# TensorE passes eight stage meetings without waiting, and issues 21 idle matmuls at three waits

## What is computed

```python
h = h + 0.5 * swiglu(rmsnorm(h, g), wg, wu, wd)
h = h + even_mixer(rmsnorm(h, mix_g), ...)      # layer 0; layer 1: odd_mixer
h = h + memory_xattn(rmsnorm(h, mg), rmsnorm(mem, sg), wq, wkv, qg, kg, wo)
h = h + 0.5 * swiglu(rmsnorm(h, g2), wg2, wu2, wd2)
```

## Time and profile before

| | |
|---|---|
| median of three runs | 1660.08 us (1658.35 to 1664.02) |
| profiled execution: time, span | 1660.82 us, 1659.0 us |
| TensorE busy | 1612.4 us, 97% of the span |
| VectorE busy | 1018.5 us, 61% |
| ScalarE busy | 863.3 us, 52% |
| mean granted TensorE clock | 0.996 of full |
| chain that ended last: share of TensorE | 87% |

### The profile page before, as it was taken

One profiled execution on the slowest core, in us unless ns is written; L12 is line 12 of the kernel. 1 busy time (PEld: TensorE's weight loads), 2 busy tenths in 40 slices (PEclk: granted clock), 3 DMA queues, 4 the chain that ended last, 5 costly groups with the idle time before them and its releaser, 6 DMA issues.

```text
span 1659.0 us, 21003 instructions
## 1 busy us (share of the span) xinstructions
PE 1612.4 (97%) x8524; PEld 1364.0 (82%) x8524; DVE 1018.5 (61%) x1379; ACT 863.3 (52%) x1193; POOL 33.7 (2%) x35
## 2 busy tenths in 40 slices
PE   9989999999999999999899999999999999999998
PEld 8878877999888888877777888888888888778887
DVE  5565578698755554568866555455544775765543
ACT  5365675566545443555666444354434565654441
POOL 0000002000000000002000000000000000000000
PEclk9999999999999999999999999999999999999999
DMA  7742324765544555544243655555554533435543
GB/s 286 289 167 108 127 104 176 286 225 189 183 178 178 180 185 193 178 152 153 71 159 130 222 181 180 201 177 178 188 192 178 178 127 127 152 128 190 191 178 127
DMA packets 42959, 289.95 MB, mean 175 GB/s; under 512 B 5048, under 2 KB 5198, under 8 KB 9968
## 3 DMA queue, kind: packets, MB, share of 16 engines
q1 hardware_dynamic: 38272, 271.93, 45.5%
q0 software_dynamic: 4592, 16.69, 2.9%
HBM read 287.51 MB, written 8.55 MB: 178 GB/s over the span
## 4 chain that ended last, share of the span: by engine, by line
PE 87%; DVE 6%; ACT 3%; DMA 2%; issue 1%; DVEq 0%; PEldq 0%; SPq 0%; ACTq 0%; POOL 0%; PEld 0%
PE bank L481 26%; PE bank L483 26%; PE bank L482 25%; PE bank L487 5%; DVE low L447 2%; DMA raw<-stream_dram 2%; PE bank L763 1%; ACT high L436 1%; PE bank L1401 1%; PE bank L645 1%; DMA h<-x_dram 0%; PE bank L1989 0%; PE bank L1843 0%; DVE h L1182 0%; DVE prob L1796 0%
## 5 line engine op out<-in xcount | busy, mean ns | idle before, releaser
L447 DVE TENSOR_TENSOR low<-raw,high 128x2048 fp32r<-128x2048 f32 x254 | 581.2, 2297 | 376.6 <-ACT high L436 376.0
L436 ACT ACTIVATE high<-raw 128x2048 fp32r<-128x2048 f32 x256 | 486.9, 1913 | 350.3 <-DMA raw<-stream_dram 345.6
L481 PE MATMUL bank<-high,xh 128*128 128x512 f32 (+1 forms) x1232 | 486.1, 395 | 6.5 <-DVEq L2720 3.5
L483 PE MATMUL bank<-high,xl 128*128 128x512 f32 (+1 forms) x1232 | 477.8, 388 | 0.0
L482 PE MATMUL bank<-low,xh 128*128 128x512 f32 (+1 forms) x1232 | 477.1, 387 | 0.0
L481 PEld LDWEIGHTS bank<-high,xh 128*128 128x128 f32 x1232 | 232.1, 188 | 54.7 <-DVE low L447 4.6
L483 PEld LDWEIGHTS bank<-high,xl 128*128 128x128 f32 x1232 | 231.9, 188 | 48.4
L482 PEld LDWEIGHTS bank<-low,xh 128*128 128x128 f32 x1232 | 232.3, 189 | 44.5
L481 PE MATMUL bank<-high,hh 128*128 128x512 f32 x440 | 171.9, 391 | 0.0
L483 PE MATMUL bank<-high,hl 128*128 128x512 f32 x440 | 171.3, 389 | 0.0
L482 PE MATMUL bank<-low,hh 128*128 128x512 f32 x440 | 171.2, 389 | 0.0
(11 more groups left out here) (242 smaller groups left out, 1522.2 us busy)
## 6 DMA issues: line engine op xcount, KB each, us to landing
raw<-stream_dram SPq DMA_DIRECT2D x257, 1024.0 KB, 4.8
band_wide_dram<-band_rows_dram POOLq DMA_DIRECT2D x1, 3072.0 KB, 33.4
t_wide_dram<-t_rows_dram POOLq DMA_DIRECT2D x1, 2304.0 KB, 17.1
u<-mem_dram POOLq DMA_DIRECT2D x2, 1024.0 KB, 5.1
bias<-band_wide_dram POOLq DMA_DIRECT2D x1, 2048.0 KB, 14.3
rel_wide_dram<-rel_rows_dram POOLq DMA_DIRECT2D x1, 1920.0 KB, 17.1
bias<-t_wide_dram POOLq DMA_DIRECT2D x1, 1536.0 KB, 10.7
bias<-rel_wide_dram POOLq DMA_DIRECT2D x1, 1280.0 KB, 7.0
```

Source lines behind the costliest of these rows:

```text
L436: act.activation(self.high[:, n % RING, :], self.raw[:, n % RING, :], ACT.Copy).then_inc(self.high_split, 1)
L447: dve.tensor_tensor(self.low[:, n % RING, :], self.raw[:, n % RING, :], self.high[:, n % RING, :].bitcast(F32), ALU.subtract).then_inc(sel ...
L481: pe.matmul(out, lh, rh, start=start, stop=False)
L483: return pe.matmul(out, ll, rh, start=False, stop=stop)
```

## The change

Idle matmuls are issued on TensorE behind the latent projection (8), and in `Rope` behind the first turn (5) and the second (8).

TensorE does not wait at the meeting in front of eight stages: the seven that follow residual sums with an early turn, and the odd attention. It still drains and adds its one to `stage_done`. Instead it waits for the semaphores that it needs: that GpSimd has cleared the set (`cleared`), that the early tiles are copied (`early_low`), and behind the first `k` of products that all four quarters are summed (`sum_added`). The tiles 4 and 5 are turned behind the products of `k` = 0, tiles 6 and 7 behind those of `k` = 1. In front of the odd attention it waits for the drained rows and copies of the earlier jobs. VectorE splits the second weight slot ahead of the low halves of tiles 4 to 7. ScalarE's order is as before.

```diff
     def begin(self, pe, s):
+        if self.early:
+            return
         self.tensor(pe, s, 0, self.early + self.AHEAD)
+    def after(self, pe, s, k):
+        if self.early and 2 * k < KT - self.early:
+            if k == 0:
+                pe.wait_ge(self.core.sum_added, self.sums_needed)
+            self.tensor(pe, s, self.early + 2 * k, self.early + 2 * k + 2)
     def next(self, pe, s, k):
+        if self.early:
+            return
     def arrive(self, pe, s, k):
+        if self.early and k == 0:
+            pe.wait_ge(self.core.early_low, self.early_needed)
...
         if self.source:
+            if self.source.early:
+                c.split_low(dve, self.jobs[0][0].slot(self.jobs[0][1]) + 1 - LEAD)
             self.source.lows(dve, s)
...
+        keep_clock(pe, c, self.idle)
+        if self.leads:
+            self.rows_there(pe, s, len(self.jobs) - 2)
+            pe.wait_ge(s["turned_by_act"], self.turn.drained("act", len(self.turn.by) - 1))
...
+        core.split_low(dve, self.up.first + 1 - LEAD)
         self.rows.lows(dve, s)
-        core.split_low(dve, self.up.first + 1 - LEAD)
...
             self.turn_rows(pe, s, b)
+            keep_clock(pe, self.core, (5, 8)[b])
...
+    def meet(engine, n, wait=True):
         engine.drain().then_inc(core.stage_done, 1)
+        if not wait:
+            return
...
             for n, stage in enumerate(stages):
+                if stage.ahead:
+                    pe.wait_ge(core.cleared, n - 1)
                 stage.tensor(pe, core.sets[n % 2])
-                meet(pe, n)
+                meet(pe, n, wait=n + 1 == len(stages) or not stages[n + 1].ahead)
...
                     pool.sem_clear(range(other[0], other[-1] + 1))
+                    pool.drain().then_inc(core.cleared, 1)
```

More of the change, by code:

```diff
@@ L497 @@
 class Stage:
+    ahead = False
     def __init__(self, core):
@@ L745, in __init__ @@
         self.early = 0
+        self.sums_needed = None
         self.step = 2 if base == 0 and tiles == KT and gain is None else 1
@@ L748, in __init__, with begin_early @@
         self.gain = PARAM(core.param, "gains")[:, n:n + KT] if gain else None
-    def begin_early(self):
+    def begin_early(self, early_before, sums_needed):
         self.early, self.banks = 4, tuple(range(8))
+        self.early_needed, self.sums_needed = early_before + self.early, sums_needed
     def bank(self, k):
@@ L791, in early_lows @@
             dve.wait_ge(s["next_high"], k + 1)
-            self.low(dve, k).then_inc(s["next_low"], 1)
+            self.low(dve, k).then_inc(self.core.early_low, 1)
     def tensor(self, pe, s, first=0, end=KT):
@@ L952, in __init__ @@
     def __init__(self, core, x, jobs, loads=None, source=None, scale=False, batches=None,
-                 masked=0, select=None, ending=False, by_act=(), behind=()):
+                 masked=0, select=None, ending=False, by_act=(), behind=(), idle=0):
         super().__init__(core)
+        self.idle = idle
         self.ending = len(jobs) - 1 if ending else None
@@ L960, in __init__ @@
         self.select = select
+        self.leads = False
         self.masked = masked
@@ L986, in tensor @@
         xh, xl = self.x
-        if self.source:
+        if self.source and not self.source.early:
             self.source.tensor(pe, s)
@@ L1003, in tensor @@
                     c.release(last, m, i0 + j)
+                if self.source and n == 0:
+                    self.source.after(pe, s, k)
                 if self.select:
@@ L1015, in tensor @@
             self.turn.turn_rows(pe, s, len(self.jobs) - 1)
+        keep_clock(pe, c, self.idle)
+        if self.leads:
+            self.rows_there(pe, s, len(self.jobs) - 2)
+            pe.wait_ge(s["turned_by_act"], self.turn.drained("act", len(self.turn.by) - 1))
+            if self.shared:
+                pe.wait_ge(s["turned_by_dve"], self.turn.drained("dve", len(self.turn.by) - 1))
     def scalar(self, act, s):
@@ L1100, in gpsimd @@
                 cut, _ = self.quarter(b, half)
-                pool.wait_ge(s["rows_added"], n + 1)
+                pool.wait_ge(c.sum_added, self.sums_before + n + 1)
                 pool.dma_start(self.store[:, b, cut], c.h[:, b, cut]).then_inc(c.stored, 16)
@@ L1131, in tensor @@
             if n == 2 and self.following:
-                pe.wait_ge(s["rows_added"], 2)
+                pe.wait_ge(c.sum_added, self.sums_before + 2)
                 self.following.early_tensor(pe, s)
@@ L1182, in vector @@
             dve.scalar_tensor_tensor(c.h[:, b, cut], ps, self.row_factor(b), c.h[:, b, cut], ALU.mult, ALU.add)\
-               .then_inc(s["rows_added"], 1)
+               .then_inc(c.sum_added, 1)
     def add_normed(self, dve, s, last):
@@ L1422, in tensor @@
                 core.release(last, self.up, i)
+                if c == 0:
+                    self.rows.after(pe, s, k)
                 if k == KT // 2 - 1 and c:
@@ L2604, in first_mixer @@
                    [(m, 0, (0, 1), 384, [u[:, b, 1200:1584] for b in range(NB)]),
-                    (m, 2, (2,), HALF, [u[:, b, 1584:2096] for b in range(NB)])], by_act=(0,), behind=(0, 1)),
+                    (m, 2, (2,), HALF, [u[:, b, 1584:2096] for b in range(NB)])], by_act=(0,), behind=(0, 1), idle=8),
            Rope(c, turned, lambda b: u[:, b, 1200:1584], lambda b: u[:, b, 1584:2096], lambda b: u[:, b, 1168:1200],
@@ L2703, in stages_of @@
                       store=out.rearrange("a (b p) d -> p (a b) d", p=P) if layer else None))
+    sums = early = 0
+    for stage in st:
+        if isinstance(stage, Residual) and stage.gain is None:
+            stage.sums_before = sums
+            sums += len(stage.order)
     for stage, then in zip(st, st[1:]):
@@ L2707, in stages_of @@
             assert stage.following.rows is c.h
-            stage.following.begin_early()
+            stage.following.begin_early(early, stage.sums_before + len(stage.order))
+            early += stage.following.early
+            then.ahead = True
+        if isinstance(stage, Project) and isinstance(then, Attention) and len(stage.jobs) > 2 and not stage.select:
+            stage.leads = then.ahead = True
     return st
@@ L2716, in program @@
     numbers = [sorted(x.num for x in s.values()) for s in core.sets]
-    def meet(engine, n):
+    def meet(engine, n, wait=True):
         engine.drain().then_inc(core.stage_done, 1)
+        if not wait:
+            return
         engine.wait_ge(core.stage_done, 4 * (n + 1))
```

3 lines of the change are left out of this document (2 added, 1 removed).

## The result

| | before | after |
|---|---|---|
| median of the runs, measured side by side (20 each) | 1663.38 us | 1668.13 us |
| ratio, 95% interval | | 1.0034 (1.0023 to 1.0045) |
| profiled execution: time, span | 1660.82, 1659.0 us | 1671.25, 1669.5 us |
| mean granted clock of the profiled execution | 0.996 | 0.989 |

A forecast was written before the change was run, and what follows sets the result against it. TensorE, busy for 97% of the span, was taken as the bound. Wait and idle-matmul terms of +0.9 and clock +2.0 on the profiled 1660.82 gave 1663.7, or 1663.0 us for the median; range 1655.5 to 1667.5.

The forecast's parts named there:

- The meeting: At eight meetings TensorE still drains; next work starts 0.23 us behind its last, so first products come 0.69 or 0.75 earlier.
- Rival 4: New waits hold TensorE as the meeting did; no gain, the squares' delay of 1.8 + 0.95 remains: 1662.9 us, chance 0.08.
- The squares: Behind the meetings, ScalarE's squares of the norm begin 1.8 us later, and root, inverse and weight slot splits move with them.
- M: The old start of the turn of rows behind a meeting; squares were at M + 1.89, forecast at M + 3.7.
- The query projections: Memory query projections end later: second layer +1.8 us, first layer +0.95, with rests of 3.7 and 2.7 us behind them.
- Rival 1: The squares' delay is hidden and each meeting gives its full 0.7 us: 1654.4 us, chance 0.13.
- The other stages: Three feed-forwards -0.75 us in all, odd projection 0, even projection -0.7, odd attention -0.5.
- The idle matmuls: They lie inside three waits, but TensorE may be last at the meeting behind the third: +0.1 us, bounds 0 and +0.3.
- Rival 2: Idle matmuls or changed phase remove first-mixer clock falls, and rival 1's gains come in part: 1659.0 us, chance 0.14.
- The clock: Falls in the long rests behind the query projections, about 2 us each: +2.0 us, bounds 0 and +5.
- the likeliest case: One clock fall behind the two query projections' rests, +2.0 us; chances 2 in 3 for the longer, 1 in 2 the shorter.
- Rival 3: The clock falls in both rests behind the query projections, each costing 2 to 3 us: 1665.0 to 1667.0, chance 0.25.

The follow-up runs named there:

- squares first: The change, but ScalarE takes the squares of the norm before it copies tiles 4 to 7; 1659.94 us, 0.9989 against the kernel before.
- query as before: The change, but both memory query projections wait at their meeting and turn all tiles at once, with VectorE's old order; 1661.05 us, 1.0004 against the kernel before.
- rests filled: The change plus 18 and 28 idle matmuls behind the products of the two memory query projections; 1663.66 us, 1.0013 against the kernel before.
- the change again: The whole change once more with nothing edited, on the same chip as three other kernels; 1667.8 us, 1.0025 against the kernel before.
- meetings only: The change without its 21 idle matmuls; 1666.83 us, 1.0034 against the kernel before.

## Why the prediction was wrong

**The meeting.** Right: the gap is 0.26 us in both query projections, 0.23 was forecast. Rival 4, that the new waits hold TensorE as the meeting did, fell by this.

**The squares.** Right. The last product before them ends at 1408.72 (1408.98 less 0.26); the old turn began 0.92 behind that point, so M is 1409.64, and the squares at 1413.42 are M + 3.78. Before they were M + 1.89. That is 1.9 us later; 1.8 was forecast. The experiment "squares first" shows that this and not the lost meeting was at work: the same eight meetings, another order on ScalarE, and the loss is gone.

**The query projections.** Right in both: +1.87 for +1.8 and +0.96 for +0.95, with rests of 3.58 and 2.51 for 3.7 and 2.7. In the first layer the root's wait went from 0.83 to 0.23, the cover that was named. Rival 1 fell by this.

**The other stages: the first term that failed.** The six stages besides the query projections were forecast at -1.95 us and gave -0.5 in the profiled execution. New waits of 0.24, 0.25 and 0.22 us stand at the second chunks of the feed-forwards, where 0.3 to 0.4 was forecast. The mechanism was right; but -0.25 was booked in each, and they gave -0.04, -0.13 and +0.10. In the odd projection the wait is 0.58 and the stage lost 0.31, at its upper bound, where 0 stood. The odd attention gave 0.51, as forecast. The even projection kept its 0.77, but the even attention behind it gave 0.54 of it back at its first wait for VectorE (timeline of after; 0.87 before):

```profile
784.94 1.14 PE L488 MATMUL bank<-t 64*128 64x256 f32 x8 [1.41 <-DVE nmax L1834]
```

The prediction did not follow the gain into the next stage. In "query as before", "rests filled" and the change again the same wait is 1.41 as well. "Query as before", which has these six stages and the old query projections, is at +0.8 (0.4) at equal clock, against +1.0 (0.4) for the idle matmuls alone: together the six are worth half a microsecond in the traces and nothing that the runs can tell.

**The idle matmuls.** The forecast place is confirmed: behind the third wait TensorE is itself last at the meeting (the earlier trace rows had 1.11 there):

```profile
102.87 0.47 PE L482 MATMUL bank<-high,xh 128*128 128x512 f32 x1 [0.23 <-PEq L2767]
```

Their cost at equal clock is +1.0 us (standard error 0.4), for +0.1 with an upper bound of 0.3. At the third wait the traces show less: from 99.9 to 102.9 us the change loses 0.06 us on before and the idle matmuls alone 0.07. So whether the bound is too low stays open. Rival 2 had nothing for it: the falls at the `Compress` matmuls stand in after as in before (clock 0.75 and 0.74 from 120 to 140 us).

The sum of the wait terms was forecast at +0.9. It is +2.05 in the profiled execution and +2.4 (0.5) at equal clock.

**The clock** is the other term, and the one the likeliest case hung on. In the profiled execution it failed: +8.45 us and not +2.0. One fall of 2 us was forecast, behind one of the two rests. Such falls exist; the longer rest's cost 2.43 us, within the 2 to 3 of rival 3, and the shorter one's 1.27, less than that. In the first trace both came, and a fall in another place besides: in the even attention, between 805.9 and 819.6 us, worth 4.75 us. It is in two of three traces of the change, in the one of the change without idle matmuls, and in none of three of before. The longest rest of that attention is 1.48 us, at its start, and is as long in the kernel before. Whether the fall belongs to the change, by the shift of TensorE's phase, or is chance stays open: "query as before" and "rests filled" have the same even projection and attention and show no fall there, and the third trace of the change has none. Over all runs what goes with the clock is +2.5 (0.8) and +3.4 (1.0) us in the two kernels with both rests, where +2.0 was forecast. So the average is nearer to the forecast than the first trace; with these errors it can't be told whether the one fall of the likeliest case is what it consists of.

Together: +0.9 and +2.0 were forecast, +2.4 and +2.5 to +3.4 were measured over the runs. The miss that is clear of the errors is in the waits: 1.5 us of gains that did not come. The rest of the distance to 1668.13 is the kernel before itself, 3.3 us above the median that the forecast was put on.

Rival 3 (both rests fall, slower by over 0.3%, chance 0.25) is the case that came closest, with 1665 to 1667. It holds on average but not in each execution: with both rests present, both fell once in the three traces of the change, only the second fell once and neither once; in "meetings only" both fell. The Trainium skill's "TensorE: Matmul & The Clock Gate", "Part 4: PE-mode transpose" says that the full clock does not engage for transposes, because they don't count as busy as matmuls do, which would lengthen both rests in every run. Two of the three traces speak against that as a rule (rows 855.32, 1421.86 and 855.62, 16 transposes in 2.32 us behind rests of 2.51 and 3.58, at clock 1.00); the falls in the others agree with it.

Two numbers of the prediction's working had no rows ahead of it: the wait of 0.64 us between the two of 1.30 and 1.11, and VectorE's 0.91 us in front of the odd attention. The trace of before has both, and neither carried a large term.

## What to carry to other kernels

A wait that is taken from the bounding engine is worth what the engine behind it leaves of it: look at who reads the work that is reordered with it, and put that engine's own critical step (here the squares) ahead of what it does for convenience. Of eight waits of 0.92 or 0.98 us, 7.6 us in all, of which the forecast took 5.8 for winnable, none was left, because the engine that splits the next weights started its chain 1.9 us later. Follow a gain into the stage behind it before it is booked. And a rest made longer is not free even where the clock holds in one trace: judge it by the mean clock of many runs. Where two traces of one kernel differ through the clock, compare a stretch in which neither fell; here it agreed to 0.03 us between executions.

## What was not expected of the hardware

The same program with the same waits, equal to the hundredth of a microsecond, gets its clock falls in other places from one execution to the next, as the table of falls shows; the transposes behind one and the same wait take 2.32 us or 3.65 us. The mean granted clock of the kernel before lay at 0.9955 over its 67 runs with a clock on record and goes with three quarters of the variance of their times (1657.46 to 1668.44 us), at 1.20 us for each 0.001. The first profiled execution of the change, at 0.989 where its runs' mean was 0.993, is therefore not its typical one, and a difference of 10 us between two traces was 5 us between the medians.
